# VectorE's dependent operations separated by a drain of the engine where a semaphore count stood

## The reference, cut to what matters

```
mod = silu(c) @ w_ada + b_ada                       # shifts, scales, gates
h = LN(x) * (1 + sc_a) + sh_a
proj = h @ w_in                                     # q, k, v of both head groups
o_na   = 8 heads of neighbourhood attention on an 8 x 64 grid, with a learned bias
o_diff = 4 heads of differential attention: (softmax(s0) - lam * softmax(s1)) @ v, RMSNorm per head
x = LN(ALPHA * x + (1 + g_a) * (concat(o_na, o_diff) @ w_out))
u = LN(x) * (1 + sc_f) + sh_f
# PEER retrieval, for each token and each of 8 heads:
s_half = (u @ w_query) . sub_keys                   # two rows of 128 scores
top 16 of each half -> 256 sums -> top 16 of those  -> 16 expert numbers, g = softmax of their scores
f = sum over the 8 x 16 experts of  g * gelu(expert_down[e] . u) * expert_up[e]
x = LN(ALPHA * x + (1 + g_f) * f)
```

## Time and profile before

| | us |
|---|---|
| median of three runs | 1823.0 |
| lowest and highest run | 1817.86, 1828.52 |
| profiled execution, its own time | 1825.07 |
| span of the profiled execution, first to last instruction | 1823.3 |
| busy in it: PE, DVE, POOL, ACT | 1473.1, 1116.8, 983.7, 438.7 |
| first gather starts, last of GpSimd's 1024 gather instructions ends | 316.6, 1803.5 |

### The profile page before, as it was taken

How to read it: one execution, slowest core, us unless ns; L and a number is a source line. 1 busy time by engine, 2 the same in 40 slices (tenths; PEclk the granted TensorE clock), 3 DMA queues, 4 the chain that set the end, 5 groups by cost and what they waited for, 6 DMA issues and landing times.

```text
span 1823.3 us, 14455 instructions
## 1 busy us (share of the span) xinstructions
PE 1473.1 (81%) x4072; PEld 684.6 (38%) x4072; DVE 1116.8 (61%) x2733; ACT 438.7 (24%) x1119; POOL 983.7 (54%) x1054
## 2 busy tenths in 40 slices
PE   6999988888988897766987988876787776776775
PEld 4444557534433553222432333422343322222222
DVE  5550367776666766676565667656455674577644
ACT  3111345322221322122222222212122121122111
POOL 1000000666666666666566666666676666667663
PEclk9999999999999999998899999999898999899999
DMA  9965402999999999999899999999999999999996
GB/s 308 380 236 112 162 4 46 338 366 356 371 355 392 407 373 366 368 366 364 310 359 409 378 366 376 373 358 373 376 360 357 374 361 383 372 348 374 374 378 244
DMA packets 190617, 604.97 MB, mean 332 GB/s; under 512 B 30897, under 2 KB 31305, under 8 KB 190379
## 3 DMA queue, kind: packets, MB, share of 16 engines
q0 software_dynamic: 147456, 536.94, 77.6%
q1 hardware_dynamic: 42027, 64.30, 10.5%
q10 hardware_dynamic: 1056, 2.82, 0.5%
HBM read 600.64 MB, written 3.34 MB: 331 GB/s over the span
## 4 chain that ended last, share of the span: by engine, by line
PE 34%; POOL 19%; issue 14%; DMA 13%; DVE 11%; another core or an unknown queue 6%; ACT 1%; SPq 1%; DVEq 0%; POOLq 0%; ACTq 0%
PE pair L939 17%; POOL big L681 14%; PE pair L691 9%; POOL region_v L681 5%; DMA big<-in_expert_up,expert_idx 5%; DMA region_v<-in_expert_up,expert_idx 3%; DVE big L1528 3%; PE pair L753 3%; DMA big<-in_expert_down,expert_idx 2%; DMA region_v<-in_expert_down,expert_idx 2%; PE pair L779 1%; DVE region_v L1528 1%; PE pair L718 1%; SPq L519 1%
## 5 line engine op out<-in xcount | busy, mean ns | idle before, releaser
L939 PE MATMUL pair<-big 128*128 128x512 f32 x1460 | 728.7, 625 | 196.7 <-DMA big<-in_expert_up,expert_idx 93.3
L1528 DVE CUSTOM_DVE_ANT_0 big<-big,pair 128x1024 f32<-128x1024 f32 x363 | 441.2, 1219 | 267.0 <-DMA big<-in_expert_down,expert_idx 176.6
L939 PEld LDWEIGHTS pair<-big 128*128 128x128 f32 x1460 | 267.2, 196 | 576.2 <-issue 550.7
L681 POOL DMA_INDIRECT big<-in_expert_up,expert_idx x365 | 346.2, 949 | 247.7 <-remote 106.8
L681 POOL DMA_INDIRECT big<-in_expert_down,expert_idx x363 | 346.4, 954 | 123.6 <-issue 101.7
L939 PE MATMUL pair<-region_v,big 128*128 128x512 f32 x588 | 296.1, 625 | 78.9 <-DMA region_v<-in_expert_up,expert_idx 35.9
L1528 DVE CUSTOM_DVE_ANT_0 region_v<-region_v,pair 128x1024 f32<-128x1024 f32 x149 | 181.6, 1219 | 109.9 <-DMA region_v<-in_expert_down,expert_idx 75.2
L1163 ACT ACTIVATE big<-ident,big 128x128 f32<-128x128 f32 x512 | 163.5, 390 | 354.6 <-issue 185.4
L939 PEld LDWEIGHTS pair<-region_v,big 128*128 128x128 f32 x588 | 106.5, 196 | 228.2 <-issue 216.7
L681 POOL DMA_INDIRECT region_v<-in_expert_up,expert_idx x147 | 139.3, 947 | 95.4 <-issue 36.4
L681 POOL DMA_INDIRECT region_v<-in_expert_down,expert_idx x149 | 140.6, 944 | 52.1 <-issue 42.1
(11 more groups left out here) (156 smaller groups left out, 1078.1 us busy)
## 6 DMA issues: line engine op xcount, KB each, us to landing
big<-in_w_ada SPq DMA_DIRECT2D x8, 2048.0 KB, 22.3
big<-in_w_in SPq DMA_DIRECT2D x5, 2048.0 KB, 13.1
big<-in_w_ada SPq DMA_DIRECT2D x16, 512.0 KB, 11.9
big<-in_w_query SPq DMA_DIRECT2D x4, 2048.0 KB
big<-in_expert_up,expert_idx POOLq DMA_INDIRECT x365
big<-in_expert_down,expert_idx POOLq DMA_INDIRECT x363
big<-in_w_out SPq DMA_DIRECT2D x2, 2048.0 KB
big<-na_scr SPq DMA_DIRECT2D x24, 128.0 KB, 4.1
```

The costliest lines, as they stand in the source:

```text
L681: nc.gpsimd.indirect_dma_start(places[place], None, (expert_down if kind == "down" else expert_up)[0], bass.IndirectOffsetOnAxis(expert_id ...
L939: last = nc.tensor.matmul(pair[t % 2][:, s * HALF:(s + 1) * HALF], diag[:, j, :], places[place][:, s * HALF:(s + 1) * HALF], start=(h == 0 ...
L1528: v.tensor_tensor_reduce(out=places[place], in0=places[place], in1=u_cur[:, :], scale=1.0, scalar=0.0, op0=ALU.mult, op1=ALU.add, accum_ou ...
```

## The change

`link` no longer raises and awaits a count. It puts a drain into VectorE's instruction stream: an instruction that the engine's sequencer holds until all earlier operations of VectorE are finished, before anything behind it is issued. No other engine waited for `dve_step`.

```diff
@@ -1196,9 +1196,7 @@
             norms = [0]
 
             def link(ins):
-                steps[0] += 1
-                ins.then_inc(dve_step, 1)
-                dve.wait_ge(dve_step, steps[0])
+                nc.vector.drain()
 
             def statistics(src):
 
```

## The result

The changed kernel takes 1832.25 us (median of 9 runs, 1822.72 to 1840.28), the kernel before 1823.82 in the same comparison (9 runs). The ratio is 1.0042, interval 1.0024 to 1.0060: about 7.7 us slower (8.4 by the medians). That is clear of no change, though smaller than the 0.5% that was called measurable beforehand. All times in this document are of fast runs; the profile of e5_before is a single run, whose state isn't known. The profiled execution of the changed kernel took 1826.5 us, near the low end of its runs, so its sizes are not those of the median.

A forecast was written before the change was run, and what follows sets the result against it. GpSimd's gathers were taken to bound the loop, with VectorE partly on the chain before it. 49 links x 0.06 = 2.9 us on 1823.0 gave 1826; the forecast's own range was 1820 to 1831, over all cases 1810 to 1838.

The forecast's parts named there:

- 2 to 5 us more, loop untouched: The forecast's own case, chance 0.45: links on the chain outside the loop cost time, the loop loses nothing; likeliest 1826 us.
- What a link costs before: On VectorE, a linked operation starts 0.03 us behind its predecessor's end, an unlinked one 0.08 early: 0.11 between them.
- What a drain costs: At each VectorE link, a drain in place of the count adds +0.06 us, taken between 0.01 and 0.09.
- The lower bound: At each link, a drain ends no earlier than the linked operation starts today, so it adds at least +0.01 us.
- the upper bound: At each link, any instruction the sequencer handles between two operations costs about 0.09 us at most.
- 49 links on the chain, +2.9 us: In the attention, up to the first gathers, and after the last gather: 49 links at 0.06 us add 2.9 us.
- 583 loop links at nothing: In the loop, 35 us more VectorE time costs nothing, covered by the pace of GpSimd and the transfers.
- the light half: The half of a head without the choice's 17 links; it gives back the 1.0 us added to the other half.
- Faster by late counts: Rival, chance 0.17: in the loop counts arrive late, drains end those of 49.5 us stalls; a quarter passed on gives 1814.
- Slower by the heavy half: Rival, chance 0.18: drains cost 0.09 us or more, the half head with 17 links comes 1.5 us later; 1835 us.
- A drain does no more than the wait: Rival, chance 0.20: at every link the drain holds at the same moment, costing 0.01 us; 1823.5, no difference.
- The signs: Profile after: link gaps 0.09 us, first gather near 319, GpSimd's 1.24 us pace kept, end only as late as first gather.

The follow-up runs named there:

- e5_before: The kernel before, unchanged, profiled once more in a single run: 1826.12 us.
- e7_late_count: Kernel before, with counts in the choice of experts and layer norm awaited only ahead of the next dependent step: 1819.28 us, ratio 0.9975.
- e12_between: Kernel with late counts, one per chain of dependent steps; ahead of the first gather softmax reciprocal and choice step alternate: 1807.28 us, ratio 0.9970 against the kernel before.
- e6_extra_wait: Kernel before, with one more, already met wait behind every link's count and wait, no drain: 1824.70 us, ratio 1.0013.
- e1_pre: Kernel before, with drains only at the 150 links ahead of the loop, counts in the loop: 1815.76 us, ratio 1.0016.
- e2_loop: Kernel before, with drains only at the 602 links of the loop, counts ahead of it: 1818.31 us, ratio 1.0028.
- e9_heavy: Kernel before, counts kept, plus 256 unneeded drains, one behind each dot of a head's first half: 1817.98 us, ratio 1.0029.
- e10_light: Kernel before, counts kept, plus 256 unneeded drains, one behind each dot of a head's second half: 1814.47 us, ratio 1.0002.

## Why the prediction was right, and where it was not

The time of 1832.25 us lay in the range over all cases (1810 to 1838), 6 us above the figure, and just outside the forecast's own range of 1820 to 1831. The loss is about 7.7 us where the forecast said 2.9, and its case ("2 to 5 us more, loop untouched") is not what happened. That the time fell in the range was luck: the range is wide because it had to take in the slower rival. What the mechanism had right is the part ahead of the loop. By its steps:

- *What a link costs before: 0.03 us, 0.11 against no link.* Right. e7_late_count and e12_between turn these 0.11 into time. The rule of the Trainium skill that the forecast weighed ("VectorE: DVE Perf Modes", section "The DRAIN you can't avoid", a semaphore after each operation costs nothing extra) does not hold here where independent work can stand behind the operation: it starts 0.08 us early without the wait, and 0.25% of the time comes back.
- *What a drain costs: +0.06 us.* It is +0.04 at a plain link and +0.08 ahead of a dot, inside the bounds of 0.01 to 0.09. Ahead of the weighing it is +0.11, above them, and behind the reciprocals where the wait for TensorE had cost 0.12 it is -0.04, a small gain. Separate waits don't only narrow the cost, as I had said: 231 of the 277 stood ahead of dots, where the cost is double. The lower bound's premise, that a drain can't begin before the operation that it follows, is wrong. Its conclusion stands: the drain ends 0.03 us after that operation, and the issue of the next comes on top with 0.045. The reason for the upper bound (any instruction that the sequencer has to handle) is wrong too: at a plain link of e6_extra_wait such an instruction costs nothing.
- *49 links on the chain, +2.9 us.* e1_pre, with 45 of them, costs 2.9 us (0.2 to 5.6 by the interval). That the figures agree is in part luck. The first gather starts at 317.7, 318.6 and 318.4 in the three profiles with one drain at all those links, and at a mean of 316.7 in seven with counts (315.5 to 317.5): 1.5 us later, where the 39 links up to it at 0.06 would give 2.3. I had said near 319. One reason is the count of links: the chain of the changed kernel holds 28 drains between 255 and 329 us and 4 behind the last gather, where I had put 45 and 4. The first stretch has all 10, but from 291 us to the first gather it is 16 of 29, and behind it 2 of 6; the others stand beside other engines' pieces. The rest of e1_pre's 2.9 isn't resolved. Its second gather starts at 325.8, where the kernels with counts have 322.3 in the mean, so part may arise between the first two. The tail and the 15 links of 328 to 347 us keep their counts in e1_pre; they belong to e2_loop.
- *583 loop links at nothing.* This is the step that failed, the term that makes the difference: e2_loop gives +5.1 us (2.2 to 7.8), its 15 and 4 other links included. Of the 583 drains 159 stand on the changed kernel's chain. The cover I named, GpSimd's and the transfers' pace, is only half there. I had spread 35 us over a loop in which VectorE idles for a third, and said that the light half gives back what the heavy half takes. It does not: e9_heavy and e10_light show that drains in the first halves cost 3.6 us by the medians (5.3 by the ratio) and those in the second halves nothing that can be seen. 17 of a head's 19 or so links stand in its first half. VectorE's loop sum rises by 10 to 20 us in the three kernels with one drain at each loop link (-9, -3 and +1 against -19), and by the 5.1 us a quarter to a half of that reaches the end.
- *Faster by late counts.* Fell: the stalls are as many and as long with drains, and a drain itself lasts up to 7.5 us. What keeps VectorE from finishing there is not shown. In e9_heavy, where a drain also stands behind a dot, 29 stalls above 0.3 us stand behind those drains, and none in the kernel before behind an operation without a link.
- *Slower by the heavy half.* Its place was right, as part of what happened, its size was not. I let it start only where a half takes longer than 16 gathers; e9_heavy loses 0.29% with only some 0.9 us more in each first half (28 us over 32 heads). GpSimd's waits for dots, which I named as its sign, are 16.8 us with the change and 17.6 without, so that sign was no good. By which step VectorE's delay gets to the gathers (a place, the weights, ScalarE and TensorE behind them) no run here separates.
- *A drain does no more than the wait.* Fell: two comparisons, at +0.42% and +0.37%.
- *The signs.* The gaps, the first gather and GpSimd's pace came as forecast. "The end only as late as the first gather" did not: the first gather is 1.5 us later in the mean and the end 7.7.

## What to carry to other kernels

Average idle time of an engine doesn't cover work that is added in bursts: look at the stretch in which it is added, and test the cover by adding the same work to the busy and to the quiet stretch. A count can be raised now and awaited later, behind work that doesn't need it; a drain can't, since wherever it is put it waits for all before it. The gain at such links lay in where the wait stands (late counts: 25 us less in VectorE's loop sum, 0.25% of the time); to make it by a drain only cost.

## What the runs showed of the hardware

- A drain between two dependent operations of VectorE makes a typical gap of 0.075 us where a count raised and awaited makes 0.034; a second drain adds 0.05. A second wait that is met adds nothing to the gap at a plain link.
- Ahead of a dot the typical gap behind a drain is 0.114 us, ahead of the weighing 0.144, where behind a count they are 0.034 and 0.035.
- An operation of VectorE that waits for nothing typically starts 0.08 us before its predecessor's end.
- A drain of VectorE can last 7.5 us, 6.0 of them beyond the recorded end of the last operation ahead of it, while GpSimd goes on issuing gathers.
